# The fourth weight sum of a fast pass goes behind a later low part, and the convolution taps are split in two

## The reference, cut to what matters

```python
hn = _rmsnorm(h, pre_ffn_gain[l])
gu = hn @ w_up[l]                                  # (256, 2 * 5632)
g = _dwconv_centred(gu[..., :D_FF], ffn_conv_w[l], ffn_conv_b[l])
u = gu[..., D_FF:]
f = (jax.nn.gelu(g, approximate=True) * u) @ w_down[l]
h = h + _rmsnorm(f, post_ffn_gain[l])
```

## Time and profile before

| | |
|---|---|
| time, median of 3 runs | 2574.11 us (2573.19 to 2574.48) |
| the profiled execution | 2572.96 us, of which the span is 2571.2 us |
| PE, DVE, ACT busy | 99%, 88%, 59% of the span |
| granted PE clock, mean | 0.999 of full speed |
| the eight passes that the change touches, on PE | 1873.3 to 2046.1 us and 2229.4 to 2400.9 us |

### The profile page before, as it was taken

How to read it: one execution, slowest core, us unless ns; L and a number is a source line. 1 busy time by engine, 2 the same in 40 slices (tenths; PEclk the granted TensorE clock), 3 DMA queues, 4 the chain that set the end, 5 groups by cost and what they waited for, 6 DMA issues and landing times.

```text
span 2571.2 us, 30572 instructions
## 1 busy us (share of the span) xinstructions
PE 2554.5 (99%) x12114; PEld 2138.1 (83%) x12114; DVE 2253.4 (88%) x1825; ACT 1515.2 (59%) x1401; POOL 3.5 (0%) x8
## 2 busy tenths in 40 slices
PE   9999999999999999999999999999999999999998
PEld 8888888888888888888888888888888888888887
DVE  7889999999958998779998878797799987799888
ACT  6555666567646555446565566536566555465654
POOL 0000000000000000000000000000000000000000
PEclk9999999999999999999999999999999999999999
DMA  7565555555664555555555564544455645555554
GB/s 246 178 229 175 198 184 197 195 199 194 224 218 174 203 213 199 195 196 196 205 207 194 185 229 162 173 138 176 152 197 180 213 164 213 197 212 180 197 219 141
DMA packets 71923, 497.97 MB, mean 194 GB/s; under 512 B 8183, under 2 KB 9432, under 8 KB 12648
## 3 DMA queue, kind: packets, MB, share of 16 engines
q1 hardware_dynamic: 71784, 496.06, 54.8%
HBM read 493.93 MB, written 2.10 MB: 193 GB/s over the span
## 4 chain that ended last, share of the span: by engine, by line
PE 92%; DVE 4%; issue 1%; ACT 1%; DMA 1%; SPq 0%; DVEq 0%; ACTq 0%
PE acc L2905 29%; PE acc L2912 14%; PE acc L2847 9%; PE acc L2930 9%; PE acc L2924 9%; PE acc L2926 9%; PE acc L2855 5%; DVE w_lo L1606 2%; PE acc L3047 1%; ACT w_hi L870 1%; PE acc L3279 1%; PE acc L3055 1%; PE aux L3361 1%; PE aux L3420 1%; PE aux L3537 1%
## 5 line engine op out<-in xcount | busy, mean ns | idle before, releaser
L870 ACT ACTIVATE w_hi<-raw 128x2048 fp32r<-128x2048 f32 (+1 forms) x499 | 954.0, 1912 | 654.8 <-PE acc L2905 248.5
L1606 DVE TENSOR_TENSOR w_lo<-raw,w_hi 128x2048 fp32r<-128x2048 f32 (+1 forms) x499 | 1135.8, 2281 | 170.1 <-ACT w_hi L870 162.9
L2905 PE MATMUL acc<-w_hi,xa 128*128 128x512 f32 x2176 | 515.8, 389 | 0.0
L2905 PEld LDWEIGHTS acc<-w_hi,xa 128*128 128x128 f32 x2176 | 408.1, 188 | 84.7
L2912 PE MATMUL acc<-w_lo,xa 128*128 128x512 f32 x1088 | 268.8, 389 | 0.0
L2847 PE MATMUL acc<-xa,w_hi 128*128 128x512 f32 x1056 | 254.1, 393 | 0.0
L2912 PEld LDWEIGHTS acc<-w_lo,xa 128*128 128x128 f32 x1088 | 204.2, 188 | 42.4
L2847 PEld LDWEIGHTS acc<-xa,w_hi 128*128 128x128 f32 x1056 | 194.9, 188 | 39.3 <-issue 0.7
L2905 PE MATMUL acc<-w_hi,hid 128*128 128x512 f32 x768 | 182.9, 390 | 0.0
L2905 PEld LDWEIGHTS acc<-w_hi,hid 128*128 128x128 f32 x768 | 143.7, 188 | 29.8
L870 ACT ACTIVATE w_hi<-w_sum 128x2048 fp32r<-128x2048 f32 x52 | 99.9, 1920 | 111.0 <-PE acc L2905 41.3
(11 more groups left out here) (447 smaller groups left out, 3571.2 us busy)
## 6 DMA issues: line engine op xcount, KB each, us to landing
raw<-in_w_in SPq DMA_DIRECT2D x158, 1024.0 KB, 4.8
raw<-in_w_gate_up SPq DMA_DIRECT2D x88, 1024.0 KB, 4.8
raw<-in_w_down SPq DMA_DIRECT2D x88, 1024.0 KB, 4.9
raw<-in_w_up SPq DMA_DIRECT2D x87, 1024.0 KB, 4.8
raw<-in_w_out SPq DMA_DIRECT2D x32, 1024.0 KB, 4.8
raw<-in_w_uq SPq DMA_DIRECT2D x3, 1024.0 KB, 4.8
h_tok<-in_x_tok SPq DMA_DIRECT2D x1, 2048.0 KB, 9.3
raw<-in_w_ukv SPq DMA_DIRECT2D x4, 512.0 KB, 3.7
```

The source lines that it names most:

```text
L870: act.activation(hi_part(u, run)[:, 0:kt * P], raw_of(u)[:, 0:kt * P], ACT.Copy).then_inc(hi_made, splits(u, run))
L1606: dve.tensor_tensor(lo_part(u, run)[:, 0:kt * P], raw_of(u)[:, 0:kt * P], hi_part(u, run)[:, 0:kt * P], ALU.subtract).then_inc(lo_made, sp ...
L2905: last = pe.matmul(acc[:, bank(t + c)], a, w, start=(first and k == 0 and half == 0), stop=False, skip_group_check=more)
```

## The change

It only reorders instructions on DVE and ACT; none is added or removed.

- In every pass DVE makes the fourth weight sum behind the split of the ninth form (UP_1), not ahead of it.
- In passes 1 to 3 of a half `pass_taps` is cut in two: the four taps behind stay in form GATE_2, the four taps ahead go behind the split in form GM_3, ahead of the ninth form's split.
- In pass 0 the head tiles' steps go one to three forms later on both engines, and their last step (`head_low`) into pass 1.
- The last hidden tile's `last_high` (ACT) and `last_low` (DVE) go behind a split in the first down pass.

```diff
+                def last_high(i):
+                    m = GT - 4 + i
+                    act.wait_ge(op_f32, v0 + m + 1)
+                    act.activation(hid[:, m, 0:S], tmp[:, 3], ACT.Copy).then_inc(op_hi, 1)
...
-                    act.wait_ge(op_f32, v0 + m + 1)
-                    act.activation(hid[:, m, 0:S], tmp[:, 3], ACT.Copy).then_inc(op_hi, 1)
+                    if i < 3:
+                        last_high(i)
...
-                            else:
-                                head_middle()
...
-                            else:
-                                head_gelu()
...
-                            else:
-                                head_high()
+                        if form == GM_3 and p == 0:
+                            head_middle()
+                        if form == GM_7 and p == 0:
+                            head_gelu()
+                        if form == GM_4 and p == 0:
+                            head_high()
...
+                        if p == 0 and form == PLAIN_2:
+                            last_high(3)
...
-                def pass_taps(p):
-
-                    for back in (1, 0):
+                def pass_taps(p, backs=(1, 0)):
+
+                    for back in backs:
+                        if back == 0:
+                            step.wait()
...
-                        if back:
-                            step.wait()
...
-                            if p == 0:
-                                head_scaled()
-                        if form == GATE_2:
-                            if p:
-                                pass_taps(p - 1)
-                            else:
-                                head_taps()
-                        if form == GM_3:
-                            weight_sum(u, 4)
+                        if form == GATE_2 and p:
+                            pass_taps(p - 1, (1,))
+                        if form == GM_6 and p == 0:
+                            head_scaled()
+                        if form == GM_3:
+                            if p:
+                                pass_taps(p - 1, (0,))
+                        if form == GM_2:
+                            weight_sum(u, 4)
+                            if p == 0:
+                                head_taps()
...
-                            else:
-                                head_product()
...
-                                head_low()
+                                head_product()
+                        if form == UP_2 and p == 1:
+                            head_low()
...
-                last_low(3)
...
+                        if form == PLAIN_2 and p == 0:
+                            last_low(3)
```

## The result

The changed kernel takes 2579.65 us (median of 11 runs, 2578.49 to 2581.16) against 2573.04 us (11 runs, 2572.45 to 2574.48) for the one before on the same chip: a ratio of 1.0026, 95% interval 1.0018 to 1.0035. It is 6.6 us slower where +4.2 was forecast. That lies in the stated range, but just beyond the 0.2% that the forecast held it most likely to stay within, and at the very end of the +1.5 to +6.5 us that it called its own. The profiled execution has a span of 2578.1 us, 6.9 more than that of before.

What follows compares the result with a forecast made beforehand. PE, busy 2554.5 of 2571.2 us, was taken to bound the kernel. Passes 1 to 3 +7.0, pass 0 -0.9 and -0.5, down passes -0.3 and -1.1 gave +4.2 on 2574.1: 2578.3 us, range 2573.5 to 2582.

Steps and rivals of the forecast that it cites:

- the 0.2%: Whole kernel: changes within 0.2% (5.1 us) are about what measurement can't tell from none; chance of staying within 0.61.
- the +1.5 to +6.5 us: Whole kernel: the band of slowdown counted as the forecast's own, 74 in 100, of which 20 lie above 5.1.
- GM_2's stall: Passes 1 to 3, GM_2's low matmuls: the 0.56 us gap goes wholly, -0.42 us in each of six passes.
- The fourth sum comes 3.3 us later and makes GM_4 wait: Passes 1 to 3: GM_4's high and low parts come late, costing 1.53 us; a pass ends 1.11 us later.
- The gap at the next GM_1: Start of passes 2 and 3: GM_1's split is late, a gap of 0.2, or some 0.08 us.
- The state copy: ACT's copy of GM_7's state ends just when PE's loads ask for it; 0 to 0.1 us a pass, none taken.
- Nothing piles up from pass to pass: Passes 1 to 3: DVE catches up where it idled before and waits for ACT again at GM_7.
- Pass 0 and the down passes: Pass 0: -0.9 and -0.5 us in the two halves; down passes: -0.3 and -1.1 us.
- the end of "passes 1 to 3": Close of that step: later waits were called hidden except GM_1's; the step summed to +7.0 us.
- the lateness spreads: Rival: close calls go wrong, each costing 0.3 in six passes; + 5 us on the forecast, 2583; 11 in 100.
- three places with thin margins: ACT's state copy, GM_1 of the next pass, and GM_2 with 0.15 us to spare; three margins under 0.25 us.
- PE's clock falls: Rival: short pauses set PE to 1.2 GHz over even one pass, some 40 us more, 2618; 1 in 100.

Runs made afterwards that it cites:

- e7: Kernel before, passes 1 to 3 only: sum in GM_3, taps ahead in GM_2, GELU in GM_7, sum over hid behind the up_sums; 2570.19 us against 2572.79.
- e1: Changed kernel with the fourth weight sum put back into GM_3, behind GM_7's split and ahead of the four taps ahead; 2580.88 us, ratio to before 1.0029.
- e2: Kernel before with only the fourth sum moved behind UP_1's split in all eight passes; 2576.64 us, ratio to before 1.0014.
- e3: Changed kernel with DVE's sum over hid in pass 3 put behind that pass's two up_sums; 2576.04 us, ratio to before 1.0012.

## Why the forecast was right, and where it was short

- **GM_2's stall goes, 0.42 us a pass.** Shown: its low matmuls start at 1985.44, 2.72 behind the product before, and e7 has this gain in every pass and no other (2.7 us by the matmuls of its trace, 2.6 by its time).
- **The fourth sum comes 3.3 us later and makes GM_4 wait, 1.53 us.** Shown, to a few hundredths, at 1.50 (PE starts UP_1 0.39 us earlier than before and UP_2 1.11 later): the sum at 1991.07 (forecast 1991.06), ACT at 1993.39 (1993.39), DVE at 1995.34 (1995.36), PE's low loads at 1997.68 (1997.69), UP_2 at 1998.73 (1998.73). Gaps of 1.11 and 0.64 were put at about 1.1 and 0.5. e1 and e2 add what the forecast only implied: neither move alone makes PE wait at GM_4.
- **The rest of the pass.** The gap at the next GM_1 is 0.21 (forecast 0.2). The state copy came just in time, at no cost; e1 shows what stood behind that margin, 2.29 us of PE once the GELU comes 2 us later.
- **Nothing piles up from pass to pass.** Right: the changed kernel's passes behind pass 0 are 44.2 us each, and its GM_2 has no gap. But it holds because GM_2's split has the taps ahead out of its way; in e2, where they stay, the lateness of one pass reaches GM_2 of the next (0.79 for 0.56).
- **Pass 0 and the down passes.** Right in kind, and within 0.1 us but for the second half's down passes, -0.85 for -1.1: M_3's gap went from 0.94 to 0.69, where I had about 0.5 of it going. DVE's split of M_2 there, in the timeline:

```profile
2469.56 2.29 DVE L1613 TENSOR_TENSOR w_lo<-raw,w_hi 128x2048 fp32r<-128x2048 f32 x1 [1.00 <-ACT w_hi L870]
```

  With PE's lag of 7.59 us at this point taken off, that is 2461.97, against 2462.81 before: 0.84 us earlier, and not the 1.1 on which the forecast went. It waits for ACT's copy.
- **The step that failed is the end of "passes 1 to 3".** I followed DVE's lateness into the next pass's GM_1 and stopped there; behind pass 3 I priced it at nothing. But there the transposes for that pass (`turn_up`) stand inside the first plain unit, 3.63 us after its start, and not, as in a pass, behind two forms; they wait for all four tiles of the pass, and DVE adds the last two only after the 2.2 us sum over `hid`. Before, that had just been in time. DVE's adding and PE's loads for the transposes there:

```profile
2047.66 1.40 DVE L2638 SCALAR_TENSOR_TENSOR halves<-acc,r_ff,halves 128x512 f32<-128x512 f32 x2
2049.54 1.03 PEld L3537 LDWEIGHTS aux<-ident,halves 128*128 128x128 f32 x8
```

  The tiles were added by 2049.06, 0.48 us ahead of the loads. In the changed kernel:

```profile
2049.75 2.28 DVE L1765 TENSOR_TENSOR x_sums<-hid 128x2048 f32<-128x2048 f32 x1
2051.95 1.40 DVE L2645 SCALAR_TENSOR_TENSOR halves<-acc,r_ff,halves 128x512 f32<-128x512 f32 x2
```

  They are added by 2053.35, and the loads start at 2053.41, behind a gap of 1.64 us. That cost 1.43 and 1.44 us in the two halves, 2.9 of the 6.6. DVE adds these tiles 4.29 us later than before and PE is 2.27 us late by then, so DVE has lost 2.0 us against PE, where 0.48 was to spare. Both could be had beforehand: the margin from the trace of before, and the 2 us from the forecast's own chain (UP_2's split at 1999.35, where it stood at 1996.2, for a PE 1.11 later). e3 takes the wait away with one move on DVE.
- **The chances.** The forecast sum lay 1 us under the 0.2% mark, and "the lateness spreads" was priced at three places with thin margins. It did spread, to a fourth place that I hadn't looked at. The chance of slower, 0.32, should have been higher by what a missed consumer of a late engine is worth.

## What to carry to other kernels

An operation that makes another engine's input must be placed by its whole relay: here DVE's sum, ACT's copy, DVE's split, 6.6 us from the sum's start to PE, of which DVE can use none of the 2 us in the middle when its list has the split first. Two moves that each fit in the slack of a wait needn't fit together, and each can also block something on the relay engine (a GELU ahead of a state copy). When an engine runs later, follow it to every consumer, and at the loop's end do so again: the stage behind the loop has other waits than the next turn.

## What the runs showed of the hardware that I had not expected

In the profiled execution of e1, of six gaps of 2.3 us in the middle of UP_1, one was followed by a fall of PE's granted clock. The windows around that one and, last, around the gap of the pass behind it:

```profile
1993.00:1995.00 2.00, 1.45 (x6) 1.19 (x7) 0.97 (x1) 2.00 (x2) 0.00 (x0) 0.94 0.08 16
1995.00:1996.00 1.00, 1.00 (x4) 0.81 (x3) 0.66 (x1) 0.30 (x1) 0.00 (x0) 0.50 0.85 147
1996.00:1997.00 1.00, 1.00 (x4) 0.71 (x4) 1.00 (x1) 0.57 (x1) 0.00 (x0) 0.50 0.91 385
1997.00:1998.00 1.00, 1.00 (x4) 0.81 (x3) 1.00 (x2) 1.00 (x1) 0.00 (x0) 0.50 1.01 426
1998.00:1999.00 1.00, 1.00 (x6) 0.81 (x5) 1.00 (x2) 0.34 (x1) 0.00 (x0) 0.91 1.08 188
...
2035.00:2045.00 10.00, 8.13 (x36) 6.41 (x35) 8.63 (x9) 5.36 (x4) 0.00 (x0) 1.00 0.63 210
```

The gap ended at 1993.55. The first window's mean of 0.94 puts the fall near 1994.8; the clock is at 0.50 of full, the level of 1.2 GHz, in the next three, with PE busy all the while, and back at full early in the fourth (mean 0.91). The pass with it took 46.45 us (1993.55 to 2040.00, gap to gap) where others took 44.79: 1.7 us more. The other five gaps of the same length left the clock at 1.00, and so did all of the changed kernel's in these stages, up to 1.65 us. The rival "PE's clock falls" thus didn't come true for the change, but a variant of it with longer gaps met it, and its price was set too high: this fall lasts some 3.4 us, not a pass. It isn't the same from run to run: the mean clock of e1's 11 runs is 0.999 in six, 0.998 in four and 0.997 in one (2586.41 us), while every run of all the other kernels has 0.999. That the gaps of 2.3 us bring the falls fits all this, but nothing was run to show it, and what picks one gap of six was not tried.
